# Two projection columns, the gate chain, query blocks and chunk 0's rows move from the front of the delta block into the projection block; eight attention tiles get other times

## The chip, the cores and the metric

The kernel runs on one core of a Trainium2 chip. The metric is the device time of one execution in microseconds (us); lower is better. The core's engines each take their instructions in order: TensorE (PE) multiplies and transposes, VectorE (DVE) and ScalarE (ACT) work on rows of elements, GpSimd (POOL) does little here, and SyncE (SP) issues nearly all DMA transfers. An instruction starts when those ahead of it in its own queue have started or ended and the semaphores that it waits for have reached their values.

## The reference

One step of a hybrid decoder layer for 1024 prompt rows and 8 x 4 sample rows with 2048 cached keys each. What matters here lies between the two feed-forward parts:

```python
proj = u @ w_in
qkv_dn, z, a, b, q_sb, k_sb, v_sb = jnp.split(proj, cuts, axis=-1)
qkv_dn, new_conv = causal_short_conv(qkv_dn, conv_hist, conv_w)
...
g = -jnp.exp(a_log) * jax.nn.softplus(a + dt_bias)
beta = jax.nn.sigmoid(b)
o_dn, s_new = gated_delta_rule(q_dn, k_dn, v_dn, g, beta, s0)
o_dn = rms_norm(o_dn, dn_norm) * jax.nn.silu(z)
...
o_sb = rms_norm(stick_breaking_attention(q_sb, k_all, v_all, k_past.shape[1], sb_bias), sb_norm)
```

`a` and `b` are four columns each. The delta rule runs in chunks over the rows, with running sums G of g, exp(G), exp of the last sum of a chunk, and beta; these I call the gate factors.

## The kernel before, in words

`hymba_step` calls three blocks, one behind the other, each with its own five engine programs. All engines wait at the end of a block.

- `first_half` (L1695): the first feed-forward part, then, from about 740 us, the **projection block**: `Project` (26 units of 128 columns of `w_in`, each in three pieces of 352 rows, three matmuls per 128 rows of weights, high and low parts) and `Attend` (the prompt's stick-breaking attention, 32 tiles of one query tile and two heads) side by side. It ends at 1213.8 us.
- `delta_and_sample` (L2426), the **delta block**: the chunked delta rule over nine tiles of rows, and the samples' attention over cached pages of keys and values.
- `second_half` (L1951): the output projection and the second feed-forward part.

What sets the order: each step is a Python generator that yields a time before it issues instructions, and `interleave` (L78) always continues the generator with the smallest time. So the tables of times (`UNIT_AT`, `TILE_AT`, `piece_time` for the projection block; `PE_AT`, `DVE_AT`, `ACT_AT`, `SP_AT` with `begin(i)` and `key_time` for the delta block) only decide the place of an instruction in its engine's queue; when it runs is decided by the queue and the semaphores. A time table is not a wait.

The end of the projection block. The last units are gate units (columns of z). ACT copies a piece out of PSUM (`evacuate`), applies SiLU to the unit (`activate`, L1392, behind a table load), DVE transposes it in blocks of 32 (`turn_blocks`, L1429) and SP stores it in four transfers (`store_rows`, L1239). Behind the last unit come the columns a and b: `multiply_ab` (L1295 to L1322) multiplies them like a 27th unit, 48 matmuls of 352 columns whose weights hold the eight columns' high part and their low part, then nine transposes (L1313) bring them to rows, ACT and DVE copy and add them into the tile `ab`. The same function transposes the convolution's last rows, the tails (L1321, three groups of four), which ACT copies and SP stores (L1244). The last attention tiles run between these: for a tile the PE turns the weights (L1587), multiplies them by the values (L1603) and turns the result (L1607); DVE copies it into `o_ring` (L1692); SP stores it (L1535). Also here SP loads, for the next block, the first four key pages (`next_stage`, L1801 and L1803) and the samples' query and key columns. The block's last waits are SP's, for all stores.

The front of the delta block. SP first issues table, dt, a_log, the sample rows of a and b, bias, masks, `same_s` and `v_new` (L2544 to L2552), then pages and chunk rows, chunk 0's rows among them. DVE clears a tile for the query blocks (L3329) and copies eight blocks into it (`queries`, L3313; ACT copies the other halves), then goes through `gates` (L3067 to L3105), about 25 steps in a chain with ACT's exponentials and five small PE matmuls (L2673 to L2677); only then comes chunk 0's reduction of squares (L3113), from which the row norms and the first chunk follow. PE turns the first pages (L2814) and builds the sample masks from the bias (L2879). A page is loaded when its slot of four is free.

The delta rule's inner loops, the page rounds behind the front, and the two outer blocks are not touched.

## Time and profile before

| | us |
|---|---|
| median of 3 runs | 2350.73 (2349.08 to 2353.83) |
| span of the profiled execution | 2348.4 |
| PE busy in the span | 2249.8 (96%) |
| DVE busy | 1640.4 (70%) |
| ACT busy | 1056.3 (45%) |
| projection block, of the span | about 740 to 1213.8 |
| delta block, starts at | 1213.8 |

The profile is of one execution. In its rows PE is the matmul side of TensorE and PEld its weight loads, which overlap; "busy" does not count waits; a granted clock of 1.00 is TensorE's full speed and 0.50 half of it. Names carry a letter for their block: `a_` is first_half, `b_` and `m_` the delta block, `w_` tiles that live across blocks. On this scale a stretch in which PE is busy all the time can only shrink by taking PE's work away, while a stretch with waits can shrink by an earlier release.

### The profile page before, as it was taken

To read this page: it belongs to the slowest core of one execution; us is meant where nothing else is said; L and a number is where in the kernel's file an instruction comes from. 1 tells how busy PE (TensorE), PEld (TensorE's weight loads), DVE (VectorE), ACT (ScalarE), POOL (GpSimd) and SP (SyncE) were. 2 spreads that over 40 slices of the span, in tenths; PEclk is the share of its full clock that TensorE was granted. 3 is DMA by queue.
4 is the path that set the end of the run, shared out by engine and by line. 5 is a ranking of instruction groups with operands and counts; after the bars stand their busy time and mean duration, and the time that the engine had idled before them with its cause. 6 is when DMAs were issued, how large, how long until landed. Compare 5 with 4: busy or idle time off the path is not lost. (4 is left out here: it accounts for less than half of the span.)

```text
span 2348.4 us, 47067 instructions
## 1 busy us (share of the span) xinstructions
PE 2249.8 (96%) x18388; PEld 1997.1 (85%) x18388; DVE 1640.4 (70%) x2775; ACT 1056.3 (45%) x1935; POOL 47.9 (2%) x107
## 2 busy tenths in 40 slices
PE   7999999999999999999978899899999999999998
PEld 7999999987879888888767666577999999997786
DVE  7766766756886478676657987656676766655886
ACT  7322222234455576566655665435422323233453
POOL 0000000000000100000010001010000000000000
PEclk9999999999999999999988999999999999999999
DMA  5343343365455445344357879623143432437454
GB/s 162 104 137 119 100 137 103 117 212 187 132 178 156 115 103 107 89 106 106 72 157 272 305 266 329 200 80 126 57 153 103 134 121 85 151 117 234 133 169 152
DMA packets 390834, 345.43 MB, mean 147 GB/s; under 512 B 105593, under 2 KB 298489, under 8 KB 390672
## 3 DMA queue, kind: packets, MB, share of 16 engines
q1 hardware_dynamic: 390672, 343.21, 47.4%
q8 instruction: 109, 1.79, 0.3%
q14 instruction: 53, 0.43, 0.1%
HBM read 271.54 MB, written 88.38 MB: 153 GB/s over the span
## 5 line engine op out<-in xcount | busy, mean ns | idle before, releaser
L1268 PE MATMUL a_q<-a_uh,a_p_hi 128*128 128x352 f32 x672 | 233.9, 348 | 0.6 <-ACT a_xp L1359 0.6
L1270 PE MATMUL a_q<-a_uh,a_p_lo 128*128 128x352 f32 x672 | 216.9, 323 | 0.0
L1269 PE MATMUL a_q<-a_ul,a_p_hi 128*128 128x352 f32 x672 | 216.4, 322 | 0.0
L1268 PEld LDWEIGHTS a_q<-a_uh,a_p_hi 128*128 128x128 f32 x672 | 126.8, 189 | 23.6 <-issue 21.7
L1269 PEld LDWEIGHTS a_q<-a_ul,a_p_hi 128*128 128x128 f32 x672 | 127.4, 190 | 0.1
L1270 PEld LDWEIGHTS a_q<-a_uh,a_p_lo 128*128 128x128 f32 x672 | 126.6, 188 | 0.0
L907 PE MATMUL c_q<-c_b_hi,c_a_hi 128*128 128x512 f32 x264 | 104.8, 397 | 3.2 <-DVE c_a_lo L806 2.4
L907 PE MATMUL a_q<-a_b_hi,a_a_hi 128*128 128x512 f32 x264 | 104.2, 395 | 2.8 <-DVE a_a_lo L806 2.6
L908 PE MATMUL c_q<-c_b_hi,c_a_lo 128*128 128x512 f32 x264 | 104.1, 394 | 0.0
L909 PE MATMUL c_q<-c_b_lo,c_a_hi 128*128 128x512 f32 x264 | 103.9, 393 | 0.0
L908 PE MATMUL a_q<-a_b_hi,a_a_lo 128*128 128x512 f32 x264 | 103.4, 392 | 0.0
L909 PE MATMUL a_q<-a_b_lo,a_a_hi 128*128 128x512 f32 x264 | 103.3, 391 | 0.0
L1685 DVE TENSOR_TENSOR_SCAN a_run<-a_run,a_zeros 128x1024 f32<-128x1024 f32 (+7 forms) x64 | 84.0, 1343 | 14.3 <-ACT a_run L1630 14.1
L793 ACT ACTIVATE c_a_hi<-c_a_raw 128x512 fp32r<-128x512 f32 x66 | 41.6, 631 | 94.7 <-PE c_q L909 70.0
L793 ACT ACTIVATE a_a_hi<-a_a_raw 128x512 fp32r<-128x512 f32 x66 | 41.7, 631 | 86.8 <-PE a_q L909 74.0
L806 DVE TENSOR_TENSOR c_a_lo<-c_a_raw,c_a_hi 128x512 fp32r<-128x512 f32 x66 | 45.3, 687 | 42.9 <-ACT c_a_hi L793 42.9
L806 DVE TENSOR_TENSOR a_a_lo<-a_a_raw,a_a_hi 128x512 fp32r<-128x512 f32 x66 | 45.4, 689 | 39.9 <-ACT a_a_hi L793 39.8
L1622 ACT ACTIVATE a_ex<-a_q,a_bias 128x512 f32<-128x512 f32 (+3 forms) x96 | 50.5, 578 | 49.5 <-PE a_q L1574 46.8
L545 DVE TENSOR_TENSOR c_w_lo<-c_w_raw,c_w_hi 128x512 fp32r<-128x512 f32 x60 | 41.3, 688 | 38.7 <-ACT c_w_hi L540 38.7
L545 DVE TENSOR_TENSOR a_w_lo<-a_w_raw,a_w_hi 128x512 fp32r<-128x512 f32 x60 | 41.3, 688 | 35.0 <-ACT a_w_hi L540 35.0
L907 PEld LDWEIGHTS c_q<-c_b_hi,c_a_hi 128*128 128x128 f32 x264 | 49.5, 188 | 19.0 <-DVE c_a_lo L806 3.9
L540 ACT ACTIVATE a_w_hi<-a_s 128x512 fp32r<-128x512 f32 x40 | 25.3, 631 | 89.3 <-DVE a_s L557 79.1
(749 smaller groups left out, 7644.3 us busy)
## 6 DMA issues: line engine op xcount, KB each, us to landing
w_page<-in_cache_v SPq DMA_DIRECT2D x128, 256.0 KB, 4.3
a_w_raw<-in_ffn_gu SPq DMA_DIRECT2D x44, 512.0 KB, 5.1
c_w_raw<-in_ffn_gu SPq DMA_DIRECT2D x44, 512.0 KB, 5.0
a_a_raw<-hid_rows SPq DMA_DIRECT2D x66, 256.0 KB, 2.7
c_a_raw<-hid_rows SPq DMA_DIRECT2D x66, 256.0 KB, 2.7
k_blocks<-in_cache_k SPq DMA_DIRECT2D x64, 256.0 KB, 3.8
w_page<-in_cache_k SPq DMA_DIRECT2D x64, 256.0 KB, 4.2
w_page<-k_blocks SPq DMA_DIRECT2D x64, 256.0 KB, 5.1
```

Source lines behind the costliest of these rows:

```text
L540: self.nc.scalar.activation(self.w_hi[j][:], src, ACT.Copy).then_inc(E("w_hi"), 1)
L545: self.nc.vector.tensor_tensor(self.w_lo[j][:], src, self.w_hi[j][:].bitcast(F32), ALU.subtract).then_inc(self.E("w_lo"), 1)
L793: nc.scalar.activation(self.a_hi[s % 3][:], self.a_raw[s % 3][:], ACT.Copy).then_inc(E("a_hi"), 1)
L806: nc.vector.tensor_tensor(self.a_lo[s % 3][:], self.a_raw[s % 3][:], self.a_hi[s % 3][:].bitcast(F32), ALU.subtract).then_inc(E("a_lo"), 1)
L907: nc.tensor.matmul(out[i], ah[:, cols], bh[:], start=(k == 0), stop=False)
L908: nc.tensor.matmul(out[i], al[:, cols], bh[:], start=False, stop=False)
L909: mm = nc.tensor.matmul(out[i], ah[:, cols], bl[:], start=False, stop=(k == PAIRS - 1))
L1268: nc.tensor.matmul(self.pm[at % 2][:, 0:TB], wh, self.uh[t][:, c], start=(c == 0), stop=False)
L1269: nc.tensor.matmul(self.pm[at % 2][:, 0:TB], wh, self.ul[t][:, c], start=False, stop=False)
L1270: mm = nc.tensor.matmul(self.pm[at % 2][:, 0:TB], wl, self.uh[t][:, c], start=False, stop=(c == KC - 1))
L1622: nc.scalar.activation(self.ex[m % 2][:, e, c0:c1], self.z[e][:, 0:c1 - c0], ACT.Exp, bias=self.bias[:, 2 * hp + e:2 * hp + e + 1]).then_i ...
L1685: nc.vector.tensor_tensor_scan(r, r, self.zeros[:].broadcast_to([P, self.keys(m)]), 0.0, ALU.add, ALU.add).then_inc(E("summed"), 1)
```

## The change

1. **Columns a and b.** `multiply_ab` goes. A new class `Gates` multiplies them at the place of time 140, some 350 us earlier in the block. Its weights are 16 columns wide (eight high, eight low) and not 128; ACT copies the product from PSUM in three steps; nine matmuls against a small matrix of ones turn it into rows and add both parts at once. They use one PSUM bank, shared with the value rows' transposes.
2. **The gate chain.** All its steps move from the delta block into `Gates`, at time 156.5: DVE's and ACT's steps and the five matmuls of the sums. The results stay in a tile `held`. dt and a_log are loaded at time 74. In the projection block each step is a separate piece of the order.
3. **Query blocks.** The clear goes to POOL, and the sixteen copies on DVE and on ACT go to time 463, near the end of the projection block (class `QueryBlocks`).
4. **Loads for the delta block.** The page table is loaded at time 66 and chunk 0's rows behind the query columns in `next_stage`. The reload of `same` is gone. SP begins the delta block with bias, masks and v_new.
5. **Tails.** Their twelve transposes and the store move to time 425 and following, ahead of the last units.
6. **Waits.** The attention's stores are no longer waited for at the end of the projection block but in `attended`, in front of the transfer that reads them. `first_half` uses one semaphore in place of several for its reciprocals.
7. **Times of the last eight tiles.** The last eight values of `TILE_AT` become smaller, the last one by 23.45.

PE at the end of the projection block, last rows of the block. L1574 to L1607 are attention, L1313 and L1321 the columns' and the tails' transposes. Before:

```order
L1574 MATMUL a_q<-a_k_213,a_q_211 128x128 x2
L1587 MATMUL a_q<-w_ident,a_ex_228 128x128 x4
L1603 MATMUL a_q<-a_wt,a_v_218 64x128 x4
L1313 MATMUL a_q<-w_ident,a_post_214 128x16 x9
L1321 MATMUL a_q<-w_ident,a_tail 27x128 x4
L1607 MATMUL a_q<-w_ident,a_ot 128x128
L1587 MATMUL a_q<-w_ident,a_ex_229 128x128
L1321 MATMUL a_q<-w_ident,a_tail 27x128 x4
L1587 MATMUL a_q<-w_ident,a_ex_229 128x128
L1321 MATMUL a_q<-w_ident,a_tail 27x128 x4
L1603 MATMUL a_q<-a_wt,a_v_218 64x128 x2
L1607 MATMUL a_q<-w_ident,a_ot 128x128
```

After; L1280 to L1282 are the three matmuls of the last projection unit, `a_p_hi` and `a_p_lo` its weights, L1778 to L1798 attention:

```order
L1280 MATMUL a_q<-a_uh_188,a_p_hi_207 128x352
L1281 MATMUL a_q<-a_ul_191,a_p_hi_207 128x352
L1282 MATMUL a_q<-a_uh_188,a_p_lo_211 128x352
L1778 MATMUL a_q<-w_ident,a_ex_232 128x128
L1794 MATMUL a_q<-a_wt,a_v_222 64x128 x4
L1280 MATMUL a_q<-a_uh_188,a_p_hi_207 128x352
L1281 MATMUL a_q<-a_ul_191,a_p_hi_207 128x352
L1282 MATMUL a_q<-a_uh_188,a_p_lo_211 128x352
L1778 MATMUL a_q<-w_ident,a_ex_232 128x128
L1798 MATMUL a_q<-w_ident,a_ot 128x128
L1794 MATMUL a_q<-a_wt,a_v_222 64x128 x2
L1798 MATMUL a_q<-w_ident,a_ot 128x128
```

Before, the last projection matmul (L1270) stood ahead of the 48 a, b matmuls, whose last is just above these rows, and no projection matmul stands among them. Now the last one is followed only by four instructions of the last attention tile, and the transposes of columns and tails are gone from here.

DVE at the front of the delta block. `b_abx` and `b_g*` are the gate chain, `w_query_rows` the query blocks, L3236 the turns of the first pages, L3247 the scores. Before (the chain goes on for some twenty more rows):

```order
L3328 MEMSET b_abx 128x8
L3329 MEMSET w_query_rows 128x1024
L3330 MEMSET m_ones 128x128
L3313 COPY w_query_rows<-w_cols 64x2x4 x8
L3236 STREAM_TRANSPOSE w_turned_rows<-w_page_49 128x512 x2
L3319 COPY b_pick<-b_D 128x8
L3320 COPY b_row_bias<-b_D 128x1
L3236 STREAM_TRANSPOSE w_w_early<-w_page_50 128x512 x2
L3247 TENSOR_SCALAR b_ex<-b_S,b_row_bias 128x128 x2
L3067 COPY b_abx<-w_ab 128x64
L3069 TENSOR_TENSOR b_gx<-b_abx,b_dt 128x36
L3070 TENSOR_SCALAR b_ge<-b_gx 128x36
```

After, with the same page turns at L3350 and the scores at L3361; L3228 is chunk 0's reduction of squares:

```order
L3431 MEMSET b_norm 128x8
L3350 STREAM_TRANSPOSE w_turned_rows<-w_page_49 128x512 x2
L3422 COPY b_pick<-b_D 128x8
L3423 COPY b_row_bias<-b_D 128x1
L3350 STREAM_TRANSPOSE w_w_early<-w_page_50 128x512 x2
L3361 TENSOR_SCALAR b_ex<-b_S,b_row_bias 128x128 x2
L3228 TENSOR_REDUCE b_norm<-b_sc 128x8
L3229 TENSOR_SCALAR b_norm<-b_norm 128x8
```

Between the scores' copy and the reduction nothing stands any more.

SP across the change of blocks. L1801 and L1803 load pages 2 and 3, L1535 stores an attention tile, L1239 the last gate unit, L1244 the tails. Before:

```order
L1801 DMA w_page_52<-k_blocks 128x512
L1535 DMA o_rows<-a_o_ring 128x128
L1239 DMA gate_rows<-a_nat 32x33x32 x4
L1535 DMA o_rows<-a_o_ring 128x128 x3
L1244 DMA out_conv_rows<-a_tail_nat 27x1536
L1702 UNCONDITIONAL_BRANCH
L2542 UNCONDITIONAL_BRANCH
L2544 DMA b_table<-in_page_table 1x128x1
L2545 DMA b_dt<-in_dt_bias 128x4
L2546 DMA b_a_log<-in_a_log 128x4
L2548 DMA b_abx<-w_ab 32x8
L2549 DMA b_bias<-in_sb_bias 8x1
```

After, with the loads at L1996 and L1998, attention's store at L1730 and the gate unit's at L1242:

```order
L1998 DMA w_page_52<-in_cache_k 128x512
L1996 DMA w_page_52<-k_blocks 128x512
L1730 DMA o_rows<-a_o_ring 128x128
L1242 DMA gate_rows<-a_nat 32x33x32 x4
L1893 UNCONDITIONAL_BRANCH
L2749 UNCONDITIONAL_BRANCH
L2751 DMA b_bias<-in_sb_bias 8x1
L2752 DMA m_masks<-mask_rows 128x768
L2753 DMA b_v_new<-out_v_rows 32x512
L2628 TENSOR_LOAD w_table
```

The gate unit's four stores are now the block's last transfers, and five transfers have left the front of the next block, four of them ahead of the bias.

DVE where the first steps of the gate chain now stand, in the projection block; `a_ab_rows` and `a_ga_steps` are the chain's tiles, L1876 attention's scans, L1845 its copies, L1450 the convolution:

```order
L1573 COPY a_ab_rows<-a_q 128x64
L1574 COPY a_ab_rows<-a_q 32x8
L1418 STREAM_TRANSPOSE a_nat<-a_post_219 128x1056
L1578 TENSOR_TENSOR a_ga_steps<-a_ab_rows,a_ga_rows 128x36
L1845 COPY a_wt<-a_q 128x128
L1876 SCALAR_TENSOR_TENSOR a_run_233<-a_run_233,a_zeros 128x512
L1581 TENSOR_SCALAR a_ga_steps<-a_ga_steps 128x36
L1876 SCALAR_TENSOR_TENSOR a_run_233<-a_run_233,a_zeros 128x512
L1845 COPY a_wt<-a_q 128x128
L1584 TENSOR_SCALAR a_ga_steps<-a_ga_steps 128x36
L1587 RECIPROCAL w_held<-a_ga_steps 128x36
L1588 SCALAR_TENSOR_TENSOR a_ga_steps<-a_ga_steps 128x36
```

The chain's steps stand singly between the steps of attention and convolution.

```diff
-TILE_AT = (76.3, 96.11, 121.61, 140.19, 151.86, 161.47, 168.08, 176.88, 182.16, 209.99, 220.74, 235.76, 247.15, 255.21, 263.73, 271.33, 276.97, 297.86, 311.81, 326.94, 337.11, 350.07, 366.34, 375.69, 379.43, 401.07, 418.96, 444.21, 458.65, 466.83, 481.74, 489.45)
+TILE_AT = (76.3, 96.11, 121.61, 140.19, 151.86, 161.47, 168.08, 176.88, 182.16, 209.99, 220.74, 235.76, 247.15, 255.21, 263.73, 271.33, 276.97, 297.86, 311.81, 326.94, 337.11, 350.07, 366.34, 375.69, 377.4, 396.5, 412.5, 430.5, 443, 452, 460.5, 466)
...
+TAIL_ROWS_AT = 425.0
...
-    def multiply_ab(self, pe):
...
-            for c in range(KC):
-                nc.tensor.matmul(self.pm[at % 2][:, 0:TB], self.w_hi[z][:, c * P:(c + 1) * P], self.uh[t][:, c], start=(c == 0), stop=False)
-                mm = nc.tensor.matmul(self.pm[at % 2][:, 0:TB], self.w_hi[z][:, c * P:(c + 1) * P], self.ul[t][:, c], start=False, stop=(c == KC - 1))
...
+    def turn_tail(self, pe):
...
         for b in range(3):
...
+            yield TAIL_ROWS_AT + 4.0 * b
...
+class Gates:
...
+    SPLIT_AT, MULTIPLY_AT, CHAIN_AT = 74.0, 140.0, 156.5
...
+        for t in range(3):
+            yield self.MULTIPLY_AT + 5.0 * t
+            if t == 0:
+                pe.wait_ge(*self.made("split"))
+                pe.wait_ge(pr.E("evacuated"), 6)
+            else:
+                pe.wait_ge(*self.made(f"cols{t - 1}"))
+            for c in range(KC):
+                if c > 0:
+                    yield self.MULTIPLY_AT + 5.0 * t + 0.5 * c
+                nc.tensor.matmul(self.bank[0:16, 0:TB], self.w[:, c, :], pr.uh[t][:, c], start=(c == 0), stop=False)
+                mm = nc.tensor.matmul(self.bank[0:16, 0:TB], self.w[:, c, :], pr.ul[t][:, c], start=False, stop=(c == KC - 1))
+            mm.then_inc(E("tensor"), 1)
...
+        for i in range(NT + 1):
+            n = P if i < NT else T_S
+            mm = nc.tensor.matmul(self.rows[0:n, 8 * i:8 * i + 8], self.cols[:, i * P:i * P + n], self.fold[:], start=True, stop=True)
...
+class QueryBlocks:
...
+    AT = 463.0
...
+    def clear(self, pool):
+        self.nc.gpsimd.memset(self.query[:], 0.0).then_inc(self.cleared, 1)
...
-                sp.dma_start(early_cols[:], project.qk_cols).then_inc(early_in, 16)
+                sp.dma_start(early_cols[:], project.qk_cols).then_inc(queries.E("cols_in"), 16)
+                project.wait_rows(sp)
+                sp.dma_start(rows0[:], project.qkv_nat[0:P, :]).then_inc(rows0_in, 16)
...
             project.wait_stores(sp)
-            attend.wait_stores(sp)
...
         @block.sync
         def _(sp):
-            sp.dma_start(table[:].rearrange("o (p b) -> o p b", b=N_B), page_table.rearrange("b (o p) -> o p b", o=1), allow_slow_non_contiguous=True).then_inc(E("table_in"), 16)
-            sp.dma_start(dt[:], dt_row.partition_broadcast(P)).then_inc(E("gate_in"), 16)
-            sp.dma_start(a_log[:], a_log_row.partition_broadcast(P)).then_inc(E("gate_in"), 16)
-            sp.wait_ge(E("abx_zero"), 1)
-            sp.dma_start(abx[0:T_S, NT, :], ab[P - T_S:P, NT, :]).then_inc(E("gate_in"), 16)
             sp.dma_start(bias[:], bias_row.rearrange("(h o) -> h o", o=1)).then_inc(E("bias_in"), 16)
             sp.dma_start(masks[:].rearrange("p n c -> p (n c)"), mask_rows).then_inc(E("delta_in"), 16)
-            sp.dma_start(same_s[:], same_rows).then_inc(E("delta_in"), 16)
             sp.dma_start(v_new[:], v_rows[T_P:T, :]).then_inc(E("v_new_in"), 16)
-            sp.wait_ge(E("table_in"), 16)
...
             def chunk_rows():
-                for i in range(3):
+                for i in range(1, 3):
...
             def attended():
                 yield begin(1) + SP_AT["attended"][0]
+                for stored in attended_out:
+                    sp.wait_ge(stored, 16 * Attend.COUNT // 4)
...
-            interleave(queries(), masks_of_samples(), chain(), advance(), gates(), norms(), prepare(), key_copies(), logits(), weigh(), keep(), finish())
+            nc.vector.memset(norm[:, NT, :], 1.0).then_inc(E("norm_set"), 1)
+            dve.wait_ge(E("norm_set"), 1)
+            interleave(masks_of_samples(), chain(), advance(), norms(), prepare(), key_copies(), logits(), weigh(), keep(), finish())
```

## Rows read from the trace of the kernel before

**Rows 1.** The page's first line: length of the profiled execution.

```profile
span 2348.4 us, 47067 instructions
```

**Rows 2.** Busy time by stretch: length; PE, PEld, DVE, ACT, POOL; clock; DMA share.

```profile
844.00:870.00 26.00, 24.09 (x175) 20.89 (x174) 25.00 (x42) 16.05 (x27) 0.00 (x0) 1.00 0.56 121
1209.00:1213.80 4.80, 0.00 (x0) 0.00 (x0) 0.29 (x1) 0.00 (x0) 0.00 (x0) 0.77 0.15 48
1213.80:1221.00 7.20, 4.55 (x23) 3.85 (x27) 6.41 (x17) 4.25 (x13) 3.12 (x9) 0.50 0.32 89
1223.60:1231.40 7.80, 3.54 (x21) 3.44 (x22) 4.36 (x24) 1.40 (x9) 3.51 (x7) 0.82 0.63 236
```

**Rows 3.** Waits of PE, 1100 to 1209 us: total us, times, longest.

```profile
PE a_q L1603 <- ACT a_wt L1652: 3.1, 4, 1.1
PE a_q L1587 <- DVE a_wt L1654: 2.4, 1, 2.4
...
PE a_q L1587 <- DVE a_ex L1559: 0.2, 1, 0.2
```

**Rows 4.** Waits of PE, 820 to 900 us, first and last of four.

```profile
PE a_q L1603 <- DVE a_o_ring L1692: 1.7, 1, 1.7
...
PE a_q L1603 <- ACT a_wt L1652: 0.5, 1, 0.5
```

**Rows 5.** Timeline of PE: start, length, engine, line, tiles, shape, count, [idle before].

```profile
1189.94 0.41 PE L1306 MATMUL a_q<-a_uh,a_p_hi 128*128 128x352 f32 x1
...
1192.67 1.09 PE L1603 MATMUL a_q<-a_wt,a_v 128*64 128x128 f32 x16
...
1205.19 0.73 PE L1313 MATMUL a_q<-w_ident,a_post 16*128 16x16 f32 x9
1205.85 0.62 PE L1321 MATMUL a_q<-w_ident,a_tail 128*27 128x128 f32 x4
...
1218.39 0.55 PE L2879 MATMUL b_D<-b_bias,b_pick_t 8*128 8x1 f32 x2 [2.61 <-DMA b_bias<-in_sb_bias]
...
1227.87 0.38 PE L2673 MATMUL b_D<-m_g,m_masks 128*128 128x32 f32 x2 [4.61 <-DVE b_gm L3089]
...
1229.17 1.97 PE L2814 MATMUL b_S<-w_ident,w_page 128*128 128x128 f32 x8
...
1246.61 1.04 PE L2814 MATMUL b_S<-w_ident,w_page 128*128 128x128 f32 x8
```

**Rows 6.** Timeline of SP's issues, 1190 to 1217 us.

```profile
1191.33 0.36 SPq L1803 DMA_DIRECT2D w_page<-in_cache_k  x1
...
1195.09 0.43 SPq L1801 DMA_DIRECT2D w_page<-k_blocks  x1
...
1196.92 3.40 SPq L1239 DMA_DIRECT2D gate_rows<-a_nat  x4
...
1209.78 0.35 SPq L1244 DMA_DIRECT2D out_conv_rows<-a_tail_nat  x1
...
1216.26 1.06 SPq L2549 DMA_DIRECT2D b_bias<-in_sb_bias  x1
```

**Rows 7.** Timeline of DVE, 1195 to 1262 us.

```profile
1195.09 1.27 DVE L1429 STREAM_TRANSPOSE a_nat<-a_post 128x1056 f32<-128x1056 f32 x1
...
1223.34 0.35 DVE L3247 TENSOR_SCALAR b_ex<-b_S,b_row_bias 128x128 f32<-128x128 f32 x1 [0.52 <-PE b_S L2826]
...
1232.15 1.22 DVE L3113 TENSOR_REDUCE b_norm<-b_sc 128x8 f32<-128x1024 f32 x1 [0.77 <-ACT b_sc L2916]
...
1260.75 1.38 DVE L3313 COPY w_query_rows<-w_cols 64x8 f32<-64x8 f32 x8
```

**Rows 8.** Timeline of ACT at the last gate unit.

```profile
1191.00 1.28 ACT L1392 ACT_TABLE_LOAD   x1
1192.29 1.08 ACT L1392 ACTIVATE a_post<-a_post 128x1056 f32<-128x1056 f32 x1
```

**Rows 9.** Stores of the last gate unit, 1150 to 1260 us: issue to landing.

```profile
DMA to landing us min/median/max: 2.4/3.4/4.1
```

485 lines of the change are left out of this document (271 added, 214 removed).

## Prediction

> **What bounds the kernel now.** I read four views: the busy time by stretch, the waits of TensorE (PE), the timelines of PE and VectorE (DVE) around 1209 us, and SyncE's (SP) issues there. The profiled execution spans 2348.4 us [rows 1]; the median of the runs shown is 2350.73 us, 2.3 us more, so I sum against the span and add 2.3 at the end. The change touches two blocks. In the projection block (to 1213.8 us) PE is the bound: in 1100 to 1209 us it waited in five rows for 7.8 us in all, the longest being attention's copies on ScalarE (ACT) and DVE [rows 3], and in 820 to 900 us in four rows for 4.7 us [rows 4]. The rest is work, so what is added to PE before the block's last projection matmul costs its own length, and what fills a wait costs nothing.
>
> The front of the delta block is another regime. PE stands idle from 1209.0 to 1213.8, where the new block's first instructions start [rows 2]; SP's last store of the old one is issued at 1209.78 [rows 6]. Then PE waits 2.61 us for the bias rows, which SP issues only at 1216.26 behind four other transfers, and 4.61 us for the gate chain's DVE steps [rows 5, 6]. DVE reaches the first chunk's reduction of squares, behind which chunk 0 and the later pages queue, at 1232.15, that is 18.3 us after the block's start [rows 7].
>
> **Part 1: the front of the delta block (gain).** The clear, the ones, the first eight query copies and all gate steps leave DVE's queue here, the query copies and eight gate steps leave ACT's, five small matmuls leave PE's, and table, dt, a_log, abx, same_s and rows 0 leave SP's. What is then late next is the bias: SP issues it first, and it took 1218.39 - 1216.26 = 2.1 us to reach PE. From that PE instruction (the sample masks' bias, L2879) to the end of the second score copy on DVE (1223.34 + 0.35) old and new queues hold the same work, 5.3 us [rows 5 to 7]. So the reduction can start 2.1 + 5.3 = 7.4 us after the block's start instead of 18.3: 10.9 us. Its inputs are there: chunk 0's rows were loaded in the block before, and ACT has only the table load and four page copies ahead of the square. Behind the reduction the orders are equal, so the whole block moves by this much; the page loads move too, since each is issued when its slot comes free, and SP loses the transfers ahead of them. The second query group's eight copies, 1.38 us on DVE at 1260.75 [rows 7], also go: 0 if they stood in slack, 1.4 if not; I take 0.4.
>
> The granted clock was 0.50 of full speed (the 1.2 GHz level) in 1213.8 to 1221, behind PE's pause, and 0.82 in the mean of 1223.6 to 1231.4 [rows 2]. There it had come back and fell again behind the 4.61 us wait: the eight page transposes at 1229.17 took 1.97 us, those at 1246.61 1.04 us [rows 5]. With the wait gone the second fall may not come. The price is 0 (it falls all the same) to about 2.5 us (the bursts of 1229 to 1241 at full speed); I take 1.0, since a wait of about 2.5 us for the copies behind the reduction stays. The Trainium skill, "TensorE: Matmul & The Clock Gate", section "Part 1: The HAM clock gate", says that the array starts at half rate, doubles once it has been kept busy, and falls back after standing idle; the trace agrees, and by that rule alone one would count the full 2.5. The same rule speaks against the change too, since the new block end leaves PE idle longer; but the clock is already down after today's pause, so nothing more can be lost there.
>
> Gain of the front: 10.9 + 0.4 + 1.0 = 12.3 us, between 10.9 and 14.8.
>
> **Part 2: PE's work in the projection block (cost, and waits that go).** Today the last projection matmul ends where the a, b matmuls begin, at 1189.94 [rows 5]. I call that moment M. In the new order nearly all work stands ahead of M:
> - 48 a, b matmuls, moved to about 841 us. Sixteen took 1192.67 - 1189.94 = 2.73 us [rows 5], so 8.2 us. They now have 16 columns of weights instead of 128, but stream the same 352 columns: no gain.
> - Nine fold matmuls in place of the nine transposes of 0.73 us, and five matmuls of the sums, 1229.17 - 1227.87 = 1.3 us [rows 5]: 2.0 us.
> - Twelve transposes of the tails, three times about 0.6 us [rows 5]: 1.8 us.
> - The attention tiles' PE work that stands behind 1189.94 today. The stretch from there to 1209.0, where PE falls idle [rows 2], is 19.1 us, less 8.2, 0.7, 1.8 and about 2.1 of waits (most of them the copies' and outputs' of [rows 3]): 6.3 us. About 0.9 of it stays behind M: 5.4 us.
>
> So M would be 1189.9 + 17.4 = 1207.3, less the waits that vanish ahead of it. Up to 5.7 us (the 7.8 of [rows 3] less those 2.1) and 4.7 us [rows 4] can: the tiles start up to 23 us earlier and run under projection matmuls, a 512-key copy now stands ahead of a convolution on DVE (today's single 2.4 us wait), and the a, b matmuls give DVE 8 us to catch up where it lags. Against this DVE gets the gate chain in a stretch where it was busy 25.0 of 26.0 us; the chain is about 4.4 us on DVE and 1.4 on ACT [rows 2], and the sixteen query copies come on each of both near the end. I take half, 5 us: M = 1202.3. Bounds: 1 and 9 us.
>
> **Part 3: the end of the projection block (new exposed tail).** Today the last gate unit's SiLU, transpose and store are over long before attention ends. Now they are the end. Two paths run from M. On ACT and DVE: the last tile's short steps (1.4 us), table load 1.28, SiLU 1.08, transpose 1.27 [rows 7, 8], so the rows are ready at about M + 5.2. On SP: tile 30's store waits for a copy at about M + 1.1; behind it stand the loads of pages 2 and 3, which took from 1191.33 to 1195.5, 4.2 us, with 0.5 for the table value, then tile 31's store, 0.3 each [rows 6]. So the first of the four gate stores goes out at about M + 6.5, and SP is the later of the two. The four took 3.40 us, the last going out 2.8 us after the first, and landed 3.4 us after issue in the median [rows 6, 9]: M + 12.7. The block change: from the conv store's issue to the new block's start it took 1213.8 - 1209.78 = 4.0 us including its landing [rows 6], so 2.0 to 2.4 behind a landing; I take 2.1. The new start is M + 14.8 = 1217.1, or 3.3 us later than today.
>
> **Small parts.** The early table, dt and a_log loads and the POOL clear (behind the next to last unit) have no one queued behind them. SP's load of rows 0 waits for stores of a unit two units back, landed by then. The single reciprocal semaphore changes no order. The wait for attention's stores moves to where mixed is read, long after they land. Nothing for all of these.
>
> **Sum.** 3.3 - 12.3 = -9.0: span 2339.4, median about 2341.7 us.
>
> **Rivals.**
> - The waits stay (no net recovery, 1 us): M 1206.3, start +7.3, net -5.0: 2345.7. With 0 and the low gain 10.9 it is -2.6: 2348.1, no change that can be told. For it: PE waited at many small places [rows 3, 4], and query copies and two table loads crowd ACT just where the last tiles run. Against: these tiles now have matmuls to hide under.
> - All goes well (9 us recovered, clock stays up): 1198.3 + 14.8 - 1213.8 = -0.7, less 13.8: 2336.2. The clock rule above points here.
> - The front does not carry through (the change doesn't do what it says): if chunk and page work behind it is held by something that does not move, the 12.3 shrinks to the roughly 6 that pages gain on SP's issues. Net -2.7: 2348. Against: in 1223.6 to 1231.4 PE was busy for 3.54 of 7.8 us and DVE for 4.36, in 24 short steps [rows 2]; what they wait for there is the gate chain, not a load.
> - Slower: the gate chain and query copies come out on PE. DVE is in order, so a gate step that waits for ACT or PE holds the scans and weight splits behind it, in a stretch where DVE had 1 us in 26 free [rows 2]. If the chain's 4.4 and 1.4 us and the two sets of sixteen copies (about 5 us) all become PE waits and only 2 us are recovered, M is 1207.3 + 8.8 = 1216.1, start +17.1, net +4.8: 2355.5. It turns from gain to loss when PE's waits in the block grow by more than about 3.5 us instead of shrinking by 5.
>
> **How the numbers follow.** Forecast case (2338 to 2346) 0.57; well 0.14; waits stay or front absorbed (2346 to 2349) 0.21; slower 0.08. A measurement of this kernel tells about 0.2%, 4.7 us, from no change. Below 2346.0: the forecast case, the well case and a little of the third, 0.74. Within 4.7 us: 0.19. Slower: 0.07. The range 2336 to 2349 leaves out the slower case (0.08), the lower part of the well case and the upper edge of the third, 0.05 each: about 2 in 10.
>
> **What would show it.** Right: the first reduction about 7.5 us behind the delta block's start (today 18.3), the block's start 14 to 15 us behind the last projection matmul with SP's gate stores last, PE's waits in the block about 5 us fewer, the block's start 1 to 7 us later than today. Wrong: a reduction that waits for the square or for pages; new PE waits around 860 us or in the last 40 us; a delta block whose length shrinks by less than 10 us.

## The result, and the profile after

The changed kernel takes 2362.5 us (median of 4 runs, 2357.6 to 2367.3), the kernel before 2349.9 in the same comparison; the ratio is 1.006, with a 95% interval of 1.0041 to 1.0079. Forecast were 2341.7 and a gain of 9.0 us; measured is a loss of 12.6. The profiled execution of the changed kernel is 15.6 us longer than that of before:

```profile
span 2364.0 us, 47081 instructions
```

I read the trace at the three places that the prediction named. First TensorE's end of the projection block and its start of the delta block (timeline of PE, changed kernel):

```profile
1129.42 0.32 PE L1282 MATMUL a_q<-a_uh,a_p_lo 128*128 128x352 f32 x1
1136.23 1.65 PE L1765 MATMUL a_q<-a_k,a_q 64*128 64x384 f32 x4 [6.49 <-ACT a_ex L1813]
...
1219.29 0.43 PE L1280 MATMUL a_q<-a_uh,a_p_hi 128*128 128x352 f32 x1
1219.88 0.27 PE L1778 MATMUL a_q<-w_ident,a_ex 128*128 128x128 f32 x1
...
1235.71 1.94 PE L3004 MATMUL b_S<-w_ident,w_page 128*128 128x128 f32 x8 [13.75 <-PEq L49]
```

The last projection matmul, moment M, ends at 1219.9 and not at the forecast 1202.3 (before 1189.9, [rows 5]). The delta block starts at 1235.7, not at 1217.1. Its own part came out smaller than forecast too: the third block starts at 1514.1 against 1498.7 before, so the delta block takes 278.4 us in place of 284.8. The sum: 21.9 us later at the delta block's start and 6.4 us won in it, so 15.4 us later at the third block's start, which is nearly all of the 15.6 us on the span.

The busy time by stretch, changed kernel, shows the second thing that is new, TensorE's clock (the third column from the right):

```profile
740.00:1219.90 479.90, 461.68 (x3172) 403.98 (x3170) 304.41 (x478) 287.86 (x471) 10.47 (x33) 0.98 0.41 97
900.00:910.00 10.00, 9.99 (x50) 6.99 (x49) 3.54 (x7) 7.96 (x15) 0.00 (x0) 0.85 0.34 95
1130.00:1140.00 10.00, 3.77 (x11) 2.69 (x12) 3.73 (x5) 7.53 (x9) 0.00 (x0) 0.59 0.39 105
1140.00:1150.00 10.00, 8.27 (x60) 7.88 (x61) 8.66 (x15) 6.93 (x10) 0.00 (x0) 0.90 0.36 56
1222.00:1235.70 13.70, 0.00 (x0) 0.02 (x1) 1.57 (x2) 3.27 (x4) 0.03 (x1) 0.57 0.74 197
1280.00:1292.00 12.00, 6.85 (x166) 5.25 (x160) 4.10 (x14) 2.84 (x7) 0.00 (x0) 0.86 1.03 385
```

and the same view of the kernel before, up to its own moment M:

```profile
740.00:1189.90 449.90, 437.34 (x3029) 388.42 (x3028) 293.31 (x419) 274.81 (x427) 9.41 (x32) 1.00 0.43 101
```

So TensorE's idle time ahead of M went from 12.6 us (449.9 less 437.3) to 18.2, where I had counted on 5 us less, and its busy time by 24.3 us, where I had counted 17.4. Of these 24.3, an estimated 4.6 are the clock: two stretches at half speed, 3.4 us long behind a wait of 2.32 us at 896.8 and 5.8 us long behind the wait of 6.49 us at 1129.7, in which 1.7 and 2.9 us were lost.

The long wait. VectorE ahead of it, changed kernel:

```profile
1118.60 2.28 DVE L1876 TENSOR_TENSOR_SCAN a_run<-a_run,a_zeros 128x1024 f32<-128x1024 f32 x1
1120.80 1.25 DVE L1418 STREAM_TRANSPOSE a_nat<-a_post 128x1056 f32<-128x1056 f32 x1
1121.97 0.87 DVE L1450 TENSOR_SCALAR a_post<-a_xp,a_taps 128x1024 f32<-128x1024 f32 x2
1122.75 4.16 DVE L1448 SCALAR_TENSOR_TENSOR a_post<-a_xp,a_taps,a_post 128x1024 f32<-128x1024 f32 x6
...
1126.97 2.29 DVE L1876 TENSOR_TENSOR_SCAN a_run<-a_run,a_zeros 128x1024 f32<-128x1024 f32 x1
```

and ScalarE behind it:

```profile
1129.29 1.91 ACT L1828 ACTIVATE a_run<-a_run 128x2048 f32<-128x2048 f32 x1 [6.45 <-DVE a_run L1876]
1131.22 1.28 ACT L1383 ACT_TABLE_LOAD   x1
1132.52 1.08 ACT L1383 ACTIVATE a_post<-a_post 128x1056 f32<-128x1056 f32 x1
1133.62 1.28 ACT L1384 ACT_TABLE_LOAD   x1
1134.91 1.27 ACT L1813 ACTIVATE a_ex<-a_q,a_bias 128x512 f32<-128x512 f32 x2
```

Tile 24 has two scans of 1024 elements, one for each head. In the kernel before they stand together, 4.46 us:

```profile
1111.28 4.46 DVE L1685 TENSOR_TENSOR_SCAN a_run<-a_run,a_zeros 128x1024 f32<-128x1024 f32 x2
```

With TILE_AT[24] at 377.4 in place of 379.43 the first scan comes ahead of a block transpose and a convolution and the second behind them. ACT's decays wait for both. Behind the decays stand a unit's two table loads and its SiLU, and behind those the scores' copies, which alone free the PSUM bank that TensorE needs at 1129.7. Three in-order queues pass on one delay of 6 us.

### The profile page after: what moved, and what is told of

It reads as the page before. It is cut to its first block and busy times, and to the rows that moved or that the text cites. A ratio compares the mean times of both kernels' runs of the same rounds, so it can differ in the third digit from the quotient of the medians.

```text
span 2364.0 us, 47081 instructions
## 1 busy us (share of the span) xinstructions
PE 2259.3 (96%) x18397; PEld 2000.0 (85%) x18397; DVE 1636.7 (69%) x2774; ACT 1058.1 (45%) x1934; POOL 49.0 (2%) x108
## 5 line engine op out<-in xcount | busy, mean ns | idle before, releaser
L1280 PE MATMUL a_q<-a_uh,a_p_hi 128*128 128x352 f32 x672 | 236.7, 352 | 0.2 <-DVE a_p_lo L1426 0.2
L1282 PE MATMUL a_q<-a_uh,a_p_lo 128*128 128x352 f32 x672 | 217.7, 324 | 0.0
L1280 PEld LDWEIGHTS a_q<-a_uh,a_p_hi 128*128 128x128 f32 x672 | 127.8, 190 | 28.9 <-issue 24.2
L1282 PEld LDWEIGHTS a_q<-a_uh,a_p_lo 128*128 128x128 f32 x672 | 127.4, 190 | 0.0
L1876 DVE TENSOR_TENSOR_SCAN a_run<-a_run,a_zeros 128x1024 f32<-128x1024 f32 (+7 forms) x64 | 84.5, 1346 | 16.5 <-ACT a_run L1821 16.4
```

The source lines that it names most:

```text
L1280: nc.tensor.matmul(self.pm[at % 2][:, 0:TB], wh, self.uh[t][:, c], start=(c == 0), stop=False)
L1282: mm = nc.tensor.matmul(self.pm[at % 2][:, 0:TB], wl, self.uh[t][:, c], start=False, stop=(c == KC - 1))
L1876: nc.vector.tensor_tensor_scan(r, r, self.zeros[:].broadcast_to([P, self.keys(m)]), 0.0, ALU.add, ALU.add).then_inc(E("summed"), 1)
```

## The experiments

The spans below are of one profiled execution each; the times are medians, with the ratio to the kernel before, which ran on the same chip beside them. Medians of before were 2348.2 to 2349.9.

| kernel | time, us | ratio to before (95%) | delta block starts | its length |
|---|---|---|---|---|
| before | 2350.7 | | 1213.9 | 284.8 |
| changed | 2362.5 | 1.006 (1.0041 to 1.0079) | 1235.7 | 278.4 |
| a_tile24 | 2357.7 | 1.0033 (1.002 to 1.0046) | 1230.9 | 276.3 |
| a_tiles_old | 2350.2 | 1.0006 (0.9993 to 1.002) | 1223.6 | 277.3 |
| b_tiles_new | 2360.6 | 1.0056 (1.0039 to 1.0072) | 1223.7 | 284.1 |
| b_tile24 | 2353.1 | 1.0017 (1.0 to 1.0034) | 1218.0 | 287.3 |
| b_last7 | 2353.1 | 1.0022 (1.0007 to 1.0038) | 1218.0 | 280.7 |
| a_no_query | 2358.9 | 1.0046 (1.0029 to 1.0063) | 1231.2 | 275.1 |
| a_tiles_mid | 2357.5 | 1.0034 (1.0019 to 1.005) | 1231.5 | 274.3 |
| a_no_gates | 2335.4 | 0.9954 (0.9936 to 0.9971) | 1213.6 | 268.0 |
| a_fold_spread | 2350.8 | 1.0018 (1.0003 to 1.0033) | 1222.9 | 276.5 |
| a_rows_pool | 2345.6 | 0.9991 (0.9975 to 1.0006) | 1226.9 | 274.2 |
| a_query_pool | 2348.4 | 0.9994 (0.9978 to 1.0009) | 1225.3 | 274.7 |
| a_rows_front | 2349.9 | 0.9995 (0.998 to 1.001) | 1225.1 | 275.7 |
| b_sp | 2346.7 | 0.9988 (0.9974 to 1.0001) | 1216.2 | 283.3 |
| b_front | 2344.9 | 0.998 (0.9968 to 0.9992) | 1216.0 | 280.9 |
| b_front2 | 2342.8 | 0.9967 (0.9956 to 0.9977) | 1213.5 | 286.5 |

The start is where the block's first instructions begin. The profile of b_front2 is of its slowest execution, 2352.2 us. Three of the kernels leave work out and give other results: a_no_query, a_no_gates and a_rows_pool.

One profile is one execution, and the same instructions do not always take the same time. a_rows_pool is the same program as a_tiles_old up to its delta block, which starts 3.3 us later; b_sp and b_front are the same as the kernel before up to there and start 2.3 and 2.1 us later. The delta block of before, the same in b_tiles_new, b_tile24 and b_last7, takes 280.7 to 287.3 us, on average 284.2. That of the changed kernel, the same in six others (a_tile24, a_tiles_old, a_no_query, a_tiles_mid, a_fold_spread, a_query_pool), takes 274.3 to 278.4, on average 276.1. So a difference of some 3 us between two starts, or of 4 to 6 us between two lengths, shows nothing by itself, and the changed delta block is about 8 us shorter, of which the two profiles compared above show 6.4.

### Is it the tiles' times?

Changed kernel, tile 24 back (a_tile24):

```diff
-TILE_AT = (..., 375.69, 377.4, 396.5, 412.5, 430.5, 443, 452, 460.5, 466)
+TILE_AT = (..., 375.69, 379.43, 396.5, 412.5, 430.5, 443, 452, 460.5, 466)
```

> The changed kernel with one number put back: TILE_AT[24], the first key-and-query tile whose time was changed, is 379.43 again and not 377.4. On VectorE this puts the tile's two 1024-element scans together again; in the changed kernel a block transpose and a convolution (6.2 us) stood between them, ScalarE's decays and scores waited for the second scan, and TensorE stood idle for 6.49 us at 1129.7 and then ran at a granted clock of 0.50 for about 6 us. Theory S (this split is most of the loss): the 6.5 us wait and some 2.9 us of half clock go, at most a wait of 1 to 2 us is left there; the delta block starts about 8 us earlier, at 1227 or so, and the time is 8 us below the changed kernel's 2362.5, 2354. Rival Q (the query copies and the gate chain crowd ACT and DVE): the wait shrinks but comes back further on, no more than 3 us better. Rival W (the moved work itself costs more than counted): the same.

Changed kernel, all eight back (a_tiles_old):

```diff
-TILE_AT = (..., 377.4, 396.5, 412.5, 430.5, 443, 452, 460.5, 466)
+TILE_AT = (..., 379.43, 401.07, 418.96, 444.21, 458.65, 466.83, 481.74, 489.45)
```

> The changed kernel with all eight old values of TILE_AT. Attention's last tiles then stand again up to 23 us later in the order, behind the last projection matmul. Theory S: the split at tile 24 is gone (8 us) and about 5 us of attention's matmuls move behind the last projection matmul, under the exposed tail of the last gate unit; the delta block starts 10 to 14 us earlier than in the changed kernel (1222 to 1226), the time is 2349 to 2353. If attention's last tile, not the gate unit's stores, then ends the block, the lower gain. Rival Q: the same as with tile 24 alone or a little better, 2358. Rival (the new times were needed, since a, b no longer lie behind attention): the block ends with attention's tail, no gain over tile 24 alone.

Kernel before with the eight new ones (b_tiles_new: the last diff the other way round):

> The kernel before with the eight new values of TILE_AT and nothing else of the change. Its order on VectorE shows the same split of tile 24's two scans by a convolution. Theory S: the wait of about 6 us with the fall of the clock appears here too, without any of the moved work, in place of today's 2.4 us there: 5 to 8 us slower than before, 2356. Rival Q or W (the loss needs the moved steps): same as before within 2 us.

Tile 24 alone gave 4.8 us, not 8, and left a wait of 2.7 us at the place. All eight gave 12.3, with time and start inside what theory S expected. In the kernel before the eight numbers alone cost 12 us, more than the 5 to 8 expected. PE's waits in b_tiles_new, 1090 to 1205 us (us in total, times, longest), and the clock behind the first:

```profile
PE a_q L1574 <- ACT a_ex L1622: 6.5, 1, 6.5
```

```profile
1120.00:1130.00 10.00, 7.37 (x35) 6.17 (x36) 3.73 (x5) 6.14 (x11) 0.00 (x0) 0.66 0.30 71
```

That is the same wait without any moved work. The start of the delta block moves by 9.8 us here and by 9.7 us from before to a_tiles_old, which has all of the change but the tiles' times. Together 19.5, of the 21.9 seen. So the loss comes from the eight numbers. The rest of the change gains or loses nothing that can be told (ratio 1.0006, interval 0.9993 to 1.002), where I had forecast it to win.

Which of the eight? The kernel before with tile 24 at 377.4 alone (b_tile24):

```diff
-TILE_AT = (..., 375.69, 379.43, 401.07, 418.96, 444.21, 458.65, 466.83, 481.74, 489.45)
+TILE_AT = (..., 375.69, 377.4, 401.07, 418.96, 444.21, 458.65, 466.83, 481.74, 489.45)
```

> The kernel before with one number of the change: TILE_AT[24] is 377.4 in place of 379.43. All eight new values alone made it 12 us slower (b_tiles_new: 2360.6 against 2348.7), with one wait of 6.54 us at 1122.6 and the granted clock at 0.66 behind it. Theory S (the split of tile 24's scans is most of that): 6 to 9 us slower than before, 2355 to 2357, the 6.5 us wait is there. Rival L (the other seven, which pull attention's work ahead of the last projection matmul): within 3 us of before.

and with the other seven (b_last7: 379.43, then the seven new values):

> The kernel before with the other seven values of TILE_AT, tiles 25 to 31, and tile 24 at its old 379.43. Theory S: no wait of 6 us; 3 to 6 us slower than before, 2352 to 2354, since attention's matmuls of the last tiles now lie ahead of the last projection matmul and of the a, b matmuls, which were their cover. Rival L: 9 us or more slower, nearly all of b_tiles_new's loss.

b_last7 came out as expected. b_tile24 did not: no wait of 6.5 us, and 4.5 us slower, between its two expectations, with an interval that begins at 1.0. Each half starts the delta block 4.1 us later in its profile. PE's longest waits in 1090 to 1205 us, b_tile24:

```profile
PE a_q L1603 <- ACT a_wt L1652: 2.8, 3, 1.2
PE a_q L1268 <- ACT a_xp L1359: 2.3, 1, 2.3
```

and b_last7:

```profile
PE a_q L1574 <- ACT a_ex L1622: 2.7, 1, 2.7
```

The 6.5 us need both halves. b_tile24 has the split, and ACT's decays are as late as in b_tiles_new (1115.95 against 1115.70 us), but its TensorE comes to tile 25's scores only at 1126.73:

```profile
1115.95 1.91 ACT L1637 ACTIVATE a_run<-a_run 128x2048 f32<-128x2048 f32 x1 [6.50 <-DVE a_run L1685]
1126.73 0.92 PE L1574 MATMUL a_q<-a_k,a_q 64*128 64x384 f32 x4
```

In b_tiles_new tile 25's scores stand further ahead, so that TensorE asks for the bank while ACT is late, and starts them at 1122.63 behind the wait. The traces show that it is tile 25; no run changed tile 25 alone, and how the rest of the 12 us is shared among the other six was not tested.

### Query copies

Leaving out 15 of 16 query copies on each engine (a_no_query):

```diff
             for h in range(H_SB):
                 yield self.AT + 3.0 * gi + 0.3 * h
...
+                if gi + h:
+                    continue
```

> The changed kernel without 15 of the 16 query copies on each of DVE and ACT (left out; the samples' scores are computed from cleared query blocks). Theory S: these copies stand behind the long wait and in a stretch in which TensorE hardly waits; no more than 2 us faster than the changed kernel. Rival Q: 4 us or more faster, the waits of the last 40 us of the projection block gone.

3.6 us faster than the changed kernel, with intervals that overlap: between the two expectations. The long wait is still there (6.6 us). On the old tile times the copies went to POOL instead (a_query_pool; one behind the other, so that each is waited for):

```diff
+            queries.copy(pool)
...
-                       ... gates.act(act), queries.act(act), attend.exponentials(act), ...
+                       ... gates.act(act), attend.exponentials(act), ...
...
-                       ... gates.dve(dve, E("pool_made")), queries.dve(dve), ...
+                       ... gates.dve(dve, E("pool_made")), ...
```

> As a_tiles_old (2350.2), with the 32 query copies on POOL, which is idle, one behind the other, in place of 16 on DVE and 16 on ACT. They took 3.4 us on each of these at 1191 to 1199, between the last tiles' copies. Theory Q2 (they are on the path of the last tiles, where TensorE waited 1.17 and 2.11 us): the delta block starts 1 to 3 us earlier, 2348. Rival: their place is slack, no change; or POOL is slower than the tail allows (32 steps of over 1 us) and the block starts later.

2348.4 against 2350.2 is within the noise, and the profiled start did not move earlier. So no cost of their place is shown; the two runs leave room for some 4 us at most. POOL's 32 copies took 0.26 us each, and not the over 1 us that the rival feared.

### What the gate work costs, and why it used to cost nothing

Old tile times, and the gate work left out (a_no_gates):

```diff
     def pe(self, pe, masks_made):
+        if False:
+            yield 0.0
...
+    def dve(self, dve, masks_made):
+        yield self.CHAIN_AT
+        dve.wait_ge(self.project.E("small_in"), 80)
+        self.nc.vector.memset(self.held.whole[:], 0.5)
+        self.nc.vector.memset(self.kept.last_decay, 0.5).then_inc(self.E("vector"), len(self.VECTOR))
```

> The changed kernel with the old TILE_AT (run a_tiles_old, 2350.2), and with the gate work of the projection block left out: no a, b matmuls, no fold, no chain, no sums; one memset fills the gate factors with a constant. Theory M (the moved matmuls cost TensorE just their length: 7.8 for 48, 2.0 for the fold, 1.2 for the sums, and about 1.7 to 2.9 of half clock behind them at 860 and 890 us): the last projection matmul 12 to 14 us earlier than in a_tiles_old, delta block at 1210 to 1212, time 2337 to 2339. Rival C (the chain's steps on DVE and ACT also make waits): 16 us or more. Rival F (they fill waits): 9 us or less.

The timelines of PE around M, first a_tiles_old, then a_no_gates:

```profile
1202.53 0.41 PE L1280 MATMUL a_q<-a_uh,a_p_hi 128*128 128x352 f32 x1
1203.09 0.60 PE L1778 MATMUL a_q<-w_ident,a_ex 128*128 128x128 f32 x4
...
1220.24 0.47 PE L1798 MATMUL a_q<-w_ident,a_ot 128*128 128x128 f32 x1 [0.37 <-ACT a_ot L1852]
1223.60 1.94 PE L3004 MATMUL b_S<-w_ident,w_page 128*128 128x128 f32 x8 [2.88 <-PEq L49]
```

```profile
1192.02 0.41 PE L1280 MATMUL a_q<-a_uh,a_p_hi 128*128 128x352 f32 x1
1192.58 0.60 PE L1665 MATMUL a_q<-w_ident,a_ex 128*128 128x128 f32 x4
...
1213.56 1.94 PE L2891 MATMUL b_S<-w_ident,w_page 128*128 128x128 f32 x8 [2.86 <-PEq L49]
```

M comes 10.5 us earlier and the delta block 10.0 us. That is less than theory M's 12 to 14, more than rival F's 9 and far from C's 16, all with the spread of some 3 us between profiles. TensorE's work ahead of M is 13.0 us less (438.6 us in 740 to 1192.6, against 451.6 us in 740 to 1203.1), and its idle time 2.5 us more (14.0 against 11.5). So the gate work costs TensorE about its own length, less a few microseconds of waits that it fills, and the chain's steps on DVE and ACT make no new waits that can be seen. Now compare the stretch from M to the delta block: 23.9 us before, with 48 a, b matmuls and the transposes in it; 20.5 us in a_tiles_old and 21.0 in a_no_gates, without them. In all three attention's last tiles run there, one short step after the other (TensorE busy for 10.31 of 17.6 us in a_tiles_old, at a mean clock of 0.66):

```profile
1203.40:1221.00 17.60, 10.31 (x67) 6.25 (x65) 9.35 (x22) 10.12 (x21) 0.00 (x0) 0.66 0.80 189
```

So most of the 8.2 us of a, b matmuls seem to have filled gaps that attention's chain leaves anyway. Moved to 841 us they stand where TensorE has few: in 820 to 910 us its idle time went from 4.7 us before to 2.4 in a_tiles_old, and the rest of their length is paid. The new end holds the last gate unit's stores too, so the 3.4 us are not a pure measure of this.

The rest of the time by which a_no_gates is faster lies in the delta block: 268.0 us against 277.3, with the same instructions, on gate factors that are one constant. Its granted clock was 1.00 in all stretches of 20 us behind the first, until the last; a_tiles_old had 0.83 to 0.91 in five of its fourteen. Why is open; no run here separates the constant values from chance.

### Pulling the tail together

a_tiles_mid, four last tiles between old and new:

```diff
-TILE_AT = (..., 444.21, 458.65, 466.83, 481.74, 489.45)
+TILE_AT = (..., 444.21, 454.0, 461.0, 472.0, 479.0)
```

> The changed kernel with tiles 24 to 27 at their old times and tiles 28 to 31 between old and new (454, 461, 472, 479 in place of 458.65, 466.83, 481.74, 489.45). In a_tiles_old the last projection matmul ended at about 1203.4 and the last gate unit's stores were issued by 1216.6, but attention's last four tiles ran alone to 1221, from one short wait to the next, at a granted clock of 0.50. Theory E (the block's end is then attention's chain): the delta block starts 2 to 4 us earlier, 1220 to 1222, time 2346 to 2348. Rival (the tiles' work goes ahead of the last matmul and moves the gate unit's stores by as much): same as a_tiles_old, 2350.

7 us slower than a_tiles_old. PE's waits there, 1180 to 1232 us:

```profile
PE a_q L1794 <- ACT a_wt L1843: 5.4, 1, 5.4
PE a_q L1778 <- DVE a_ex L1750: 4.5, 1, 4.5
```

Moving four tiles by 5 to 10 units of the table made two new long waits. The theory that a somewhat earlier tail is better failed in the same way as the change itself: an earlier place in the order made TensorE wait. Both waits stand behind the same group on ScalarE as the long wait, a unit's two table loads and its SiLU. Here is the first, ahead of the weights' copy (L1843) that TensorE got at 1199.8 us; the second is at 1216.0 to 1219.7 us, ahead of the decays:

```profile
1193.72 1.28 ACT L1383 ACT_TABLE_LOAD   x1
1195.02 1.08 ACT L1383 ACTIVATE a_post<-a_post 128x1056 f32<-128x1056 f32 x1
1196.12 1.28 ACT L1384 ACT_TABLE_LOAD   x1
```

### The clock behind the fold

Times between the nine fold matmuls (a_fold_spread):

```diff
         for i in range(NT + 1):
+            yield self.MULTIPLY_AT + 15.0 + 0.5 * i
             n = P if i < NT else T_S
```

> As a_tiles_old, with the nine fold matmuls (16 rows by 8 columns) given times 0.5 apart, so that projection matmuls stand between them. In a_tiles_old, a_tile24 and a_no_query the granted clock was 0.83 in 860 to 870 us with TensorE busy all the time, right behind these nine at 864.4; before has no such fall there. Theory G (that run of tiny matmuls is what precedes the fall): no fall at 860 to 870, 1.7 us earlier from there on, time 2348.5. Rival: the fall stays, it comes from elsewhere; no change.

860 to 870 us in a_tiles_old, then in a_fold_spread:

```profile
860.00:870.00 10.00, 10.00 (x62) 9.41 (x59) 5.06 (x11) 3.36 (x9) 0.00 (x0) 0.83 0.67 151
```

```profile
860.00:870.00 10.00, 9.25 (x54) 7.11 (x52) 2.38 (x6) 1.84 (x3) 0.00 (x0) 1.00 0.20 56
```

The fall is gone in this execution, as theory G has it, and also those at 890 to 910; but PE's waits in 820 to 910 rose from 2.3 to 5.0 us, and the time did not change (2350.8 against 2350.2; 2348.5 was expected). Nor are nine fold matmuls together enough for a fall. PE's timeline has the same run of them in the changed kernel, 3 us later, and there the clock stays at 1.00:

```profile
864.36 2.10 PE L1523 MATMUL a_q<-a_ab_fold,a_ab_cols 16*128 16x8 f32 x18
```

```profile
860.00:870.00 10.00, 10.00 (x70) 8.68 (x67) 5.16 (x12) 5.27 (x8) 0.00 (x0) 1.00 0.60 142
```

Of the eight kernels that have them together, six show 0.83 to 0.86 in this stretch and two, the changed one and a_rows_pool, 1.00. So theory G's cause can be part of it, and the one execution without a fall does not show it.

### The front: do transfers pace it?

Chunks 1 and 2 filled by POOL (a_rows_pool), and, on a_query_pool, chunk 1's load first (a_rows_front):

```diff
-                for i in range(1, 3):
-                    yield SP_AT["chunk_rows"][i]
-                    sp.dma_start(rows[i][:], qkv_nat[i * P:(i + 1) * P, :]).then_inc(E(f"rows_in{i}"), 16)
...
+            for i in range(1, 3):
+                nc.gpsimd.tensor_copy(rows[i][:], rows[0][:]).then_inc(E(f"rows_in{i}"), 16)
```

> As a_tiles_old, with the loads of the rows of chunks 1 and 2 (0.79 MB each) left out of the delta block's front; POOL fills these two tiles with chunk 0's rows. In the changed kernel the lead at the front was 10.0 us at the first reduction and 5.7 us from the sixth on, with the DMA engines at a share of about 1.0 in 1256 to 1292 and page waits there. Theory D (the lead is eaten by transfers that are paced by DMA): with 1.6 MB less the page wait goes and the delta block is 2 to 4 us shorter, time 2346 to 2348. Rival P (it is PE's clock and the order): same length within 1 us, or longer if POOL's copies come late.

```diff
-SP_AT = {"pages": (0.74, 7.19), "chunk_rows": (-95.52, -10.93, 3.62, 10.18, 4.04), ...
+SP_AT = {"pages": (0.74, 7.19), "chunk_rows": (-95.52, -90.0, 3.62, 10.18, 4.04), ...
```

> As a_query_pool, with the load of chunk 1's rows (0.79 MB) issued at the delta block's start, ahead of the pages, and not among them some 15 us later. Without the loads of chunks 1 and 2 (a_rows_pool) the time fell from 2350.2 to 2345.6 and the delta block from 277.3 to 274.2 us. Theory D (the front is paced by transfers, whose engines had a share of only 0.68 in the first 20 us): 1 to 3 us shorter than a_query_pool, the page wait at 26 us gone. Rival: the pages behind the 0.79 MB come late instead, the same or 2 us longer.

Without the 1.6 MB the third reduction came at 58.4 us behind the block's start (a_tiles_old 61.0, changed kernel 64.5, before 71.2) and the time fell by 4.6 us, with intervals that overlap. That leans to D and does not show it: with all loads in place the third reduction came at 60.0 to 64.9 us in the other kernels with this delta block, and at 57.4 us in a_no_gates, and the block's 274.2 us are hardly outside their 274.3 to 278.4. Moving one load to the front changed nothing that can be told (2349.9 against 2348.4), where 1 to 3 us were expected.

### The front without the move

The kernel before with another order at the delta block's front. SP alone (b_sp, the first part of the diff), then with the chain's places (b_front, the second part), then, against b_front, two steps more (b_front2, the last part):

```diff
+            sp.dma_start(bias[:], bias_row.rearrange("(h o) -> h o", o=1)).then_inc(E("bias_in"), 16)
+            sp.wait_ge(E("abx_zero"), 1)
+            sp.dma_start(abx[0:T_S, NT, :], ab[P - T_S:P, NT, :]).then_inc(E("gate_in"), 16)
...
             sp.dma_start(a_log[:], a_log_row.partition_broadcast(P)).then_inc(E("gate_in"), 16)
+            sp.dma_start(table[:].rearrange("o (p b) -> o p b", b=N_B), ...
...
-PE_AT = {... "gates": (-43.46,), ...
-ACT_AT = {... "gates": (-30.77, -41.18), ...
-DVE_AT = {... "gates": (-45.59, -26.31, -16.57), ...
+PE_AT = {... "gates": (-57.0,), ...
+ACT_AT = {... "gates": (-59.0, -41.18), ...
+DVE_AT = {... "gates": (-59.0, -57.8, -55.5), ...
...
-DVE_AT = {... "gates": (-59.0, -57.8, -55.5), ...
+DVE_AT = {... "gates": (-59.0, -58.9, -56.5), ...
```

> The kernel before with SP's new order at the delta block's front alone (bias first, table last of six), the queues of the other engines as they were. Theory K: TensorE's wait for the bias of 2.61 us goes, the chain still starts behind the scores: 1 to 2 us earlier reduction, time 2347 to 2348, not to be told from before. Rival: the pages behind the later table cost what the bias gives.

> The kernel before with the front of its delta block reordered and nothing moved out of it: SP issues bias, a and b's sample rows, dt and a_log ahead of the table; on DVE and ACT the gate chain stands behind the first page's turn and copies and not behind the scores, on TensorE the sums behind the first scores; the a, b matmuls stay at the end of the projection block. Theory K (the front's gain does not need the move: a good half of the 10 us is queue order, and the a, b matmuls under the last tiles cost nothing there): the reduction of squares at 13 to 15 us behind the block's start in place of 18.3, the start itself unmoved, time 2344 to 2346, below both kernels. Rival (the chain only changes places with page 1's turn and scores, which are then late): within 2 us of before.

> As b_front (2344.9), with two steps more ahead of page 1's turn and scores: the masked g (gm, L3089) right behind beta, and the copies of the sums between the two scores' copies. In b_front TensorE waited 3.07 us for gm, which stood behind page 1's copies, and DVE's sums copies stood behind the second scores at 1230.2, so the reduction came at 17.2 us behind the block's start, only 1.1 earlier than before, although the chain had begun 2.5 us earlier. Theory K: reduction at 13 to 14 us, delta block 2 to 3 us shorter than b_front's 280.9 us, time 2342 to 2343. Rival: the lead is given back by the third reduction, as the pages' turns then come later; the same as b_front within 1 us.

The first reduction on DVE, b_front, then b_front2 (block starts 1216.0 and 1213.5):

```profile
1233.22 1.22 DVE L3113 TENSOR_REDUCE b_norm<-b_sc 128x8 f32<-128x1024 f32 x1 [0.77 <-ACT b_sc L2916]
```

```profile
1227.43 1.22 DVE L3113 TENSOR_REDUCE b_norm<-b_sc 128x8 f32<-128x1024 f32 x1 [0.44 <-ACT b_sc L2916]
```

17.2 and 13.9 us behind the start, against 18.3 before. b_front was expected at 13 to 15 and missed; b_front2 repaired what its trace showed and landed in the range. The times are as expected: 2344.9 and 2342.8, ratios 0.998 and 0.9967, both intervals below 1. This version is faster than both kernels, with nothing moved into the projection block.

The mechanism is shown only as far as the first reduction. That b_front won 4.8 us with a reduction only 1.1 us earlier is more than it explains; b_sp, at 0.9988 with an interval that includes 1, may mean that SP's order gives part of it. For b_front2 a delta block 2 to 3 us shorter than b_front's 280.9 was expected, and its profile, of a slow execution, has 286.5. The third reduction came at 67.9 and 68.4 us in the two, hardly earlier than with the old order (68.7 to 72.7 in the four kernels that have it). So where the time is won behind the front stays open.

## Why the prediction was wrong, point by point

- **Moment M, "I take half, 5 us".** This is the step that failed. I forecast 1202.3, it was 1219.9. The waits ahead of M did not shrink by 5 us but grew by 5.6 (12.6 to 18.2), and the clock took 4.6 more. Together that is 15.2 of the 17.6 us. The 17.6 us, with 5.9 at the front and 1.0 in the tail (both below), are the whole distance between the forecast 9.0 us of gain and the 15.6 us of loss on the span. The reason given, that "the tiles start up to 23 us earlier and run under projection matmuls", treats an earlier time as help. The runs show that the eight times are the loss: 12 us in either kernel, with one new wait of 6.5 us where tile 24's split scans meet tile 25's earlier scores. I had priced their bounds at 1 to 9 us of gain, and no end of the range held a loss.
- **The moved matmuls.** Right in size: 8.2 and 2.0 us counted, and M moved by 10.5 when they were left out. The fold measures 2.03 us where 0.7 was counted as a like exchange, and a, b 7.8 where 8.2 was. Without the tiles' new times the terms give 1189.9 + 8.2 + 2.0 + 1.8 = 1201.9, measured 1203.1, and TensorE's idle time ahead of M there is 11.5 us: one of the five recovered.
- **What the move gives up.** In part 2 the old end's waits were counted, but not that the a, b matmuls had stood in a stretch that attention's chain of short steps sets. Taking 10.7 us of matmuls out of it shortened it by 3.4 us only, with the gate unit's stores now in it.
- **Tail, M + 14.8.** Measured 15.8. The order was as forecast, with SP's four gate stores last (the issue of the four, timeline of SP, changed kernel); they took 4.75 us in place of 3.40.

```profile
1226.25 4.75 SPq L1242 DMA_DIRECT2D gate_rows<-a_nat  x4
1235.67 0.34 SPq L2751 DMA_DIRECT2D b_bias<-in_sb_bias  x1
```

- **Front, 10.9 us at the first reduction.** Right: it came 8.3 us behind the start (forecast 7.4), 10.0 earlier than before.

```profile
1244.09 1.21 DVE L3228 TENSOR_REDUCE b_norm<-b_sc 128x8 f32<-128x1024 f32 x1
```

- **"Behind the reduction the orders are equal, so the whole block moves by this much".** Wrong. The lead was 10.0 us at the first reduction, 9.3 at the second, 6.7 at the third and 5.6 from the sixth on, and the block is 6.4 us shorter, not 12.3. In 1280 to 1292 us TensorE was busy for 6.85 of 12 us with the DMA engines at a share of 1.03 (row above), and at 1261.35 it had waited 1.84 us for a page. That transfers take the lead away is a guess, though. In a_tiles_old, with the same delta block, TensorE did not wait for a page there, and the lead was still 10.1 us at the third reduction and 10.3 at the ninth; yet its block is only 7.5 us shorter. Over all kernels it is about 8. So the term was too large by some 4 us, and where they go is open. The rival "the front does not carry through" had given it roughly 6.
- **Clock, 1.0 us.** The second fall of the front did not come, as hoped (0.99 in 1244 to 1260). But others came in the projection block, 4.6 us, behind a wait that was longer than before and one that was new.
- **The rivals.** The slower one, 2355.5, had the sign and not the mechanism: it put the loss on waits made by the gate chain and the query copies. The experiments show none for the first and leave room for some 4 us at most for the second. Its turning point is also off by a little: by the sum's own terms gain turns into loss when PE's waits grow by 4.0 us, not 3.5.

## What to carry to other kernels

A table of times that merges in-order queues is not smooth: 2 units on one tile moved half of a pair of scans behind a convolution, and three queues passed the delay on to TensorE. So read the new order on every engine at each changed number, price a change of order with a loss as well as a gain, and test the numbers by themselves. Work beside a chain of short steps may cost little, and the same work in a stretch where the engine is full costs its length; before moving it ask what it covers. A wait at the front of a block can sometimes be shortened by the order of its own first instructions, as here. And before a profile's difference of a few microseconds is explained, look how much two profiles of the same instructions differ.
